# Norm crossings, TensorE fillers and first mixers of a two-block transformer kernel on one core: order of VectorE, ScalarE and GpSimd work

## The reference, cut to what matters

```
xn = rms_norm(x, attn_norm);  h = xn @ w_in          # split into latent, differential, grouped parts
latent (MLA): 6 heads;  differential: 4 heads x 2 maps, o = rms_norm((p0 - lam*p1) @ v);  grouped: 6 heads
x = x + concat(o_a, o_b, o_c) @ w_o
xn = rms_norm(x, ffn_norm);   x = x + (silu(xn@wg) * (xn@wu)) @ w_down        # 2816 wide
```

```
x = layer_norm(alpha*x + mixer(x));      # neighbourhood + sliding window attention, gated
x = layer_norm(alpha*x + f(x));          # f: dense 2816 in layer 0; 8 experts of 3584, top 2, in layer 1
```

## Time and profile before

| | |
|---|---|
| Time, median of 3 runs | 2284.98 us (2283.99 to 2286.79) |
| Profiled execution | 2285.07 us, span 2283.2 us |
| Mean granted TensorE clock | 0.987 |
| TensorE / VectorE / ScalarE / GpSimd busy | 97% / 75% / 65% / 10% |
| DMA | 569.32 MB, mean 249 GB/s |
| Stretches with a low granted clock (us) | 80-86, 128-136, 432-440, 484-488, 723-730, 907-911, 1098-1102, 1276-1290 |

### The profile page before, as it was taken

How to read it: one execution, slowest core, us unless ns; L and a number is a source line. 1 busy time by engine, 2 the same in 40 slices (tenths; PEclk the granted TensorE clock), 3 DMA queues, 4 the chain that set the end, 5 groups by cost and what they waited for, 6 DMA issues and landing times.

```text
span 2283.2 us, 30956 instructions
## 1 busy us (share of the span) xinstructions
PE 2211.2 (97%) x11540; PEld 1865.9 (82%) x11540; DVE 1708.3 (75%) x2448; ACT 1481.1 (65%) x2166; POOL 229.8 (10%) x140
## 2 busy tenths in 40 slices
PE   8889999899999999999999999999999999999997
PEld 7878888787887997888889788888888888888886
DVE  6866557866556547555646799999999999999998
ACT  6655446665444564444456588777787787888886
POOL 1430000330002241000251000000000000000000
PEclk9999999999999999999999899999999999999999
DMA  7426555425555544655544599999999999999996
GB/s 286 136 82 202 186 189 197 147 67 186 186 192 172 194 139 161 195 189 185 198 148 139 187 349 371 353 358 349 363 357 367 356 359 357 365 361 375 361 374 236
DMA packets 156844, 569.32 MB, mean 249 GB/s; under 512 B 18512, under 2 KB 18864, under 8 KB 156048
## 3 DMA queue, kind: packets, MB, share of 16 engines
q1 hardware_dynamic: 153600, 554.00, 68.5%
q0 software_dynamic: 3088, 13.27, 1.7%
HBM read 566.15 MB, written 1.05 MB: 248 GB/s over the span
## 4 chain that ended last, share of the span: by engine, by line
PE 74%; DVE 3%; ACT 1%; issue 1%; POOL 0%; DVEq 0%; ACTq 0%; POOLq 0%
PE bank L510 20%; PE bank L512 20%; PE bank L511 20%; PE bank L2220 3%; PE bank L2221 3%; PE bank L2222 3%; PE bank L1808 1%; PE bank L1065 1%; PE bank L2897 1%; PE bank L1080 1%; DVE X L2091 1%; PE bank L1007 1%; PE bank L2828 1%; DVE X L2050 0%; PE bank L2876 0%
## 5 line engine op out<-in xcount | busy, mean ns | idle before, releaser
L447 DVE TENSOR_TENSOR w_lo<-raw,w_hi 128x1024 fp32r<-128x1024 f32 x987 | 1190.2, 1224 | 278.1 <-ACT w_hi L441 246.2
L441 ACT CAST w_hi<-raw 128x1024 fp32r<-128x1024 f32 x1052 | 1098.8, 1051 | 314.1 <-PE bank L512 263.6
L510 PE MATMUL bank<-w_hi,x_hi 128*128 128x512 f32 (+2 forms) x2144 | 836.7, 390 | 16.1 <-DVE x_lo L2122 7.9
L512 PE MATMUL bank<-w_hi,x_lo 128*128 128x512 f32 (+2 forms) x2144 | 826.1, 385 | 0.0
L511 PE MATMUL bank<-w_lo,x_hi 128*128 128x512 f32 (+2 forms) x2144 | 824.9, 385 | 0.0
L510 PEld LDWEIGHTS bank<-w_hi,x_hi 128*128 128x128 f32 x2144 | 405.2, 189 | 95.9 <-POOL w_lo L447 8.8
L512 PEld LDWEIGHTS bank<-w_hi,x_lo 128*128 128x128 f32 x2144 | 405.4, 189 | 79.1
L511 PEld LDWEIGHTS bank<-w_lo,x_hi 128*128 128x128 f32 x2144 | 406.0, 189 | 73.2
L447 POOL TENSOR_TENSOR w_lo<-raw,w_hi 128x1024 fp32r<-128x1024 f32 x65 | 155.3, 2394 | 577.2 <-ACT w_hi L441 572.4
L512 PE MATMUL bank<-w_hi,qk_l 128*128 128x512 f32 (+1 forms) x496 | 191.9, 387 | 0.0
L510 PE MATMUL bank<-w_hi,qk_l 128*128 128x512 f32 x448 | 178.5, 398 | 0.5 <-DVE w_lo L447 0.5
(11 more groups left out here) (280 smaller groups left out, 2017.2 us busy)
## 6 DMA issues: line engine op xcount, KB each, us to landing
raw<-in_stream SPq DMA_DIRECT2D x1052, 512.0 KB, 5.7
tab<-in_lngb POOLq DMA_DIRECT2D x5, 1024.0 KB, 7.7
arena<-in_rpb POOLq DMA_DIRECT2D x16, 256.0 KB, 6.9
tab<-in_rowv POOLq DMA_DIRECT2D x2, 640.0 KB, 10.2
X<-in_x SPq DMA_DIRECT2D x1, 1024.0 KB, 5.0
out_y<-X SPq DMA_DIRECT2D x4, 256.0 KB, 2.6
tab<-in_ropec POOLq DMA_DIRECT2D x2, 448.0 KB, 5.4
tab<-in_ropes POOLq DMA_DIRECT2D x2, 448.0 KB, 7.8
```

Of the source, the lines that this page charges most:

```text
L441: nc.scalar.copy(w_hi[:, s % SPLIT, :], raw[:, slot, :]).then_inc(hi_done, 1)
L447: e.tensor_tensor(w_lo[:, s % SPLIT, :], raw[:, s % RAW, :], w_hi[:, s % SPLIT, :].bitcast(F32), ALU.subtract).then_inc(done, 1)
L510: pe.matmul(out, xh, wh, start=first, stop=False)
L512: return pe.matmul(out, xl, wh, start=False, stop=last)
```

## The change

- `pool_halves`: GpSimd has two halves (was three) at each entry of a second mixer and one (was three) at the dense network's; VectorE splits the others.
- `crossing`: GpSimd issues one split and then the pow of row block 1, ahead of the rest; VectorE's and ScalarE's splits are placed anew, and the middle normalising step of row block 1 stands between the two x_lo units of row block 0.
- `ln_add`: one tensor_scalar in place of two small instructions.
- `keep_busy`: TensorE matmuls of identity and X (f32, 256 columns) whose result nobody reads: five after the first transposes, five (three at the router) and one or three in each `crossing`, three and one around the router's choice, six on zeros at the very start.
- Start: ScalarE runs one Square on eight columns before the inputs are there.
- First mixers: in `fill`, GpSimd waits at steps 2, 4 and 6 for the scores of the map two further on, ahead of its split; `latent_heads(0)` after the last `diff_blocks`; ScalarE takes both column evacuations and the norm products.

```diff
-        own |= set(range(mixer2_at(l), mixer2_at(l) + 3))
-    own |= set(range(mixer2_at(0) + H_MIX2, mixer2_at(0) + H_MIX2 + 3))
+        own |= {mixer2_at(l), mixer2_at(l) + 1}
+    own.add(mixer2_at(0) + H_MIX2)
...
+            if first:
+                keep_busy(E, 5, 7)
...
+        def keep_busy(E, n, b):
+            if E.kind == "pe":
+                for _ in range(n):
+                    E.e.matmul(bank[b][:, 0:S], ident[:, :], X[:, 0, 0:S], start=True, stop=True)
...
                     e.wait_ge(acc_one, E.acc.at())
+                    e.wait_ge(acc_two, E.acc.at())
                     drain_dve(E)
...
-                if hx == 2:
-                    latent_heads(0)
...
             diff_blocks(2, 0)
+            latent_heads(0)
...
-                    if E.kind == "dve":
+                    if E.kind == "act":
                         need_rs(E, rows_made["norm", h0])
-                        e.tensor_tensor(x, x, scales(at, n, DV), ALU.mult).then_inc(qk_src, 1)
-                    E.qks.n += 1
+                        for tb in range(TB):
+                            for h in range(n):
+                                j = at + tb * n + h
+                                i = nc.scalar.mul(x[:, tb, h], x[:, tb, h], rs[:, j:j + 1])
+                        i.then_inc(dn_done, 1)
...
-                if E.kind in ("act", "dve"):
+                if E.kind == "act":
                     e.wait_ge(w_used, E.st.done(-1))
...
+                    for tb, taken in enumerate((acc_one, acc_two)):
+                        nc.scalar.mul(H[:, tb, c:c + n], bank[b + tb][:, 0:n], rsx[:, tb:tb + 1]).then_inc(taken, 1)
...
+                    if E.kind == "pool" and step in (2, 4, 6):
+
+                        e.wait_ge(s_full, E.map.at(step + 2) + 1)
...
-                E.link(e.tensor_tensor(negmu[:, tb:tb + 1], sx[:, 2 * tb:2 * tb + 1], sx[:, 2 * tb + 1:2 * tb + 2],
-                                       ALU.add))
-                e.tensor_scalar(negmu[:, tb:tb + 1], negmu[:, tb:tb + 1], -1.0 / D, None, ALU.mult).then_inc(
-                    mu_ready, 1)
+                e.tensor_scalar(negmu[:, tb:tb + 1], sx[:, 2 * tb:2 * tb + 1], sx[:, 2 * tb + 1:2 * tb + 2], -1.0 / D,
+                                ALU.add, ALU.mult).then_inc(mu_ready, 1)
...
+            entered = part is not None
             if E.kind == "pool":
 
                 e.wait_ge(tp_src, E.src.at(2))
-            if E.kind != "pe" and not later:
-                for _ in range(left - 1):
+                E.half_step()
+                ln_scale(E, 1)
+                for _ in range(left - 1 + entered):
                     E.half_step()
-                if E.kind == "pool":
-                    ln_scale(E, 1)
+            if E.kind == "act":
+                E.half_step()
                 E.half_step()
-            tb_blocks(E, 0, (0, 1))
+            if E.kind == "dve":
+                if entered:
+                    E.half_step()
+                tb_blocks(E, 0, (0, 1), units=(0,))
+                if entered and left == 3:
+                    E.half_step()
+                ln_mid(E, 1)
+                tb_blocks(E, 0, (0, 1), units=(1,))
+            else:
+                tb_blocks(E, 0, (0, 1))
...
             if E.kind == "pe" and routed:
                 logits(E, 0, base)
+                keep_busy(E, 3, 2)
+            else:
+                keep_busy(E, 5, 2)
             if E.kind == "pe" and part is not None:
                 halves(0, (0, 1))
+                keep_busy(E, *idle)
             if E.kind == "act":
                 ln_scale(E, 1)
-            ln_mid(E, 1)
+                for _ in range(left - 2 + entered):
+                    E.half_step()
             ln_last(E, 1)
-            if E.kind != "pe" and part is not None or later:
-                E.half_step()
+            if E.kind == "dve":
+                for _ in range(1 + entered):
+                    E.half_step()
             tb_blocks(E, 1, (6, 7))
...
                 logits(E, 1, E.tp.at(-2)).then_inc(lg_full, 1)
+                keep_busy(E, 3, 4)
...
+                keep_busy(E, 1, 4)
...
+                e.wait_ge(warm_set, 1)
+                nc.scalar.activation(arena[:, WARM:WARM + 8], arena[:, 0:8], ACT.Square)
...
+                e.memset(arena[:, 0:WARM], 0.0).then_inc(warm_set, 1)
...
+                e.wait_ge(warm_set, 1)
+                for _ in range(6):
+                    e.matmul(bank[7][:, 0:S], arena[:, 0:P], arena[:, P:P + S], start=True, stop=True)
```

More of the change, by code:

```diff
@@ L170 @@
 assert JUNK + TB * D <= B_SS
+WARM = P + S
 E_SIL = 0
@@ L405, in build @@
         hs_src, hs_done = sem("hs_src"), sem("hs_done")
+        dn_done = sem("dn_done")
+        warm_set = sem("warm_set")
         g_divided, gt_hi = sem("g_divided"), sem("gt_hi")
@@ L1572, in column_halves @@
                 E.acc.n += 1
-                if E.kind in ("act", "dve"):
+                if E.kind == "act":
                     e.wait_ge(w_used, E.st.done(-1))
-                if E.kind == "act":
-                    nc.scalar.mul(H[:, 0, c:c + n], bank[b][:, 0:n], rsx[:, 0:1]).then_inc(acc_one, 1)
-                if E.kind == "dve":
-                    e.tensor_scalar(H[:, 1, c:c + n], bank[b + 1][:, 0:n], rsx[:, 1:2], None, ALU.mult).then_inc(
-                        acc_two, 1)
+                    for tb, taken in enumerate((acc_one, acc_two)):
+                        nc.scalar.mul(H[:, tb, c:c + n], bank[b + tb][:, 0:n], rsx[:, tb:tb + 1]).then_inc(taken, 1)
             def out_half(n, done=0):
@@ L1631, in units @@
                     if E.kind == "pe":
-                        e.wait_ge(qk_src, made["diff01"])
+                        e.wait_ge(dn_done, 2 * l + 1)
                         e.wait_ge(acc_one, E.acc.at())
@@ L1643, in units @@
                     if E.kind == "pe":
-                        e.wait_ge(qk_src, made["diff23"])
+                        e.wait_ge(dn_done, 2 * l + 2)
                     out_unit(7, 5, 2, 2 * DH, scale=og_col[:, 0:1], lag=2)
@@ L1679, in fill @@
                     diff_norm(0, 2)
-                    made["diff01"] = E.qks.at()
                 if step == 10:
@@ L1692, in fill @@
                     diff_norm(DH // 2, 2)
-                    made["diff23"] = E.qks.at()
             def rows(at, n):
@@ L1750, in out_last @@
                 E.st.s += 2
-            tail = ffn(E, FF1 // FC, TB, scaled=True, enter=lambda part: rms_crossing(
+            tail = ffn(E, FF1 // FC, TB, scaled=True, enter=lambda part, idle=None: rms_crossing(
                 E, colg[:, l, CG_FFN:CG_FFN + KD], 2, out_last, part))
@@ L1963, in part @@
                     return i
-                enter(part)
+                enter(part, idle=(3, 4))
             else:
@@ L2129, in tb_blocks, with crossing @@
                 E.tp.n += 1
-        def crossing(E, alpha, tail, part, routed=False):
+        def crossing(E, alpha, tail, part, routed=False, idle=(1, 2)):
             e = E.e
@@ L2148, in crossing @@
                 ln_add(E, 1, alpha, bank[4:8])
-            later = E.kind == "dve" and part is None
+            entered = part is not None
             if E.kind == "pool":
                 e.wait_ge(tp_src, E.src.at(2))
-            if E.kind != "pe" and not later:
-                for _ in range(left - 1):
+                E.half_step()
+                ln_scale(E, 1)
+                for _ in range(left - 1 + entered):
                     E.half_step()
-                if E.kind == "pool":
-                    ln_scale(E, 1)
+            if E.kind == "act":
                 E.half_step()
-            tb_blocks(E, 0, (0, 1))
+                E.half_step()
[9 more added lines that the diff above has]
+                tb_blocks(E, 0, (0, 1))
             def halves(tb, hs):
@@ L2171, in crossing @@
                 logits(E, 0, base)
+                keep_busy(E, 3, 2)
+            else:
+                keep_busy(E, 5, 2)
             if E.kind == "pe" and part is not None:
                 halves(0, (0, 1))
+                keep_busy(E, *idle)
             if E.kind == "act":
                 ln_scale(E, 1)
-            ln_mid(E, 1)
+                for _ in range(left - 2 + entered):
+                    E.half_step()
             ln_last(E, 1)
-            if E.kind != "pe" and part is not None or later:
-                E.half_step()
+            if E.kind == "dve":
+                for _ in range(1 + entered):
+                    E.half_step()
             tb_blocks(E, 1, (6, 7))
-            if later:
+            if E.kind == "dve" and not entered:
                 E.half_step()
@@ L3027, in entering @@
             def entering(tail, alpha):
-                return lambda part, routed=False: crossing(E, alpha, tail, part, routed)
+                return lambda part, routed=False, idle=(1, 2): crossing(E, alpha, tail, part, routed, idle)
             for l in range(LAYERS):
```

## The result

The changed kernel takes 2274.11 us (median of 5 runs, 2269.88 to 2276.85), the kernel before 2285.75 beside it (2283.99 to 2286.79): a ratio of 0.9949, with a 95% interval of 0.9936 to 0.9963, or 11.6 us less. Forecast were 24.2 us less, 2260.8. The time lies in the range given (2251 to 2275), but less than half of the gain came. The profiled execution took 2274.11, span 2272.3, granted clock 0.992.

The account below looks back on a forecast made before the run. The prediction took TensorE, busy 2211.2 of 2283.2 us, as the bound, with its idle time and low clock to win. Terms 2.8 + 2.5 + 2.5 + 3.1 + 4.0 + 6.1 + 2.8 + 0.4 = 24.2 gave 2260.8 us, range 2251 to 2275.

Parts of the forecast that it names:

- Heads of the first mixers: First mixers: with the tables behind the differential units, L1291 and the first scores come 1.8 us earlier; -5.1 us together.
- only the first softmax step's distance counts: First mixers: moved tables stand before the first softmax step; second pair's softmax starts 2.0 us earlier in layer 0.
- further gain of 1.1 us in layer 1 from the low clock at 432 us: Layer 1's first mixer: low-clock stretch 432 to 440 lies behind the wait, so 3.1 us earlier against layer 0's 2.0.
- GpSimd's new waits: First mixers, steps 2, 4, 6: splits held for scores let VectorE go first; -1.4 us a layer, -2.8.
- the split falls on the next two-input instruction instead: First mixers: the low end for GpSimd's held-back splits, where they collide with a later VectorE instruction; gain 0.
- ScalarE's evacuations and products: First mixers: column evacuations and norm products moved from busier VectorE to ScalarE; -0.5 us a layer, ends +1.0 and -1.5.
- rival B: First mixers give nothing beyond the wait, as ScalarE is late for exponentials and copies; sum 15.3, 2270 us; chance 0.20.
- Crossings 1 to 3: Crossings into both second mixers (-2.5 us each) and into the dense network (-3.1): shorter chains, fillers holding the clock.
- Crossing 4: Crossing into the experts: mainly the clock held by fillers, speeding gather, transposes and router logits; -4.0 us.
- Rival C: Clock still falls in most crossings, so only shorter chains count; sum 12.8, 2272 us; chance 0.15.
- Start: Kernel start: early table load, fillers lifting the clock, faster transposes, earlier first weight matmul; -2.8 us, +1.3 to -3.5.

Follow-up runs that it names:

- e15: e8 with the first latent tables put back ahead of the differential units; 2268.88 us (0.9933).
- e8: e2 with eight TensorE fillers in each first mixer's attention, at steps 11 and 12; 2266.85 us (0.9918).
- e5: Changed kernel keeping only the tables' new place of its four first-mixer edits; 2271.22 us (0.9940).
- e1: Changed kernel with all four first-mixer edits undone; 2273.39 us (0.9946).
- e4: Changed kernel with only the first latent tables put back ahead of the differential units; 2277.15 us (0.9969).
- e16: e8 with GpSimd's splits at steps 2 and 4 held back until VectorE's products are done; 2261.01 us (0.9887).
- e12: e8 with ScalarE's new evacuations and products given back to VectorE; 2267.09 us (0.9918).
- e11: Changed kernel, GpSimd's waits kept, with eight fillers added in each first mixer's attention; 2266.27 us (0.9913).
- e7: Changed kernel without the fillers in the crossings and at the router, those of the start kept; 2275.54 us (0.9955).
- e6: Changed kernel without the start's edits (early fillers and ScalarE table load); 2277.30 us (0.9961).
- e13: e8 with GpSimd's split at step 2 alone held back until VectorE's products are done; 2265.97 us (0.9919).
- e2: Changed kernel without GpSimd's waits for the scores in the first mixers; 2269.59 us (0.9927).

## Why the prediction was wrong, point by point

**Heads of the first mixers, -5.1: the failed step.** The price of the wait itself was right (3.7 us in two layers). What failed is the sentence that of the rest only the first softmax step's distance counts. With the scores 1.8 us earlier, GpSimd's split of step 2, which had met L1411 before, meets the product behind it: L1426 takes 2.64 us for 0.56, the two products 3.99 for 2.90, and TensorE waited 4.8 us for the split output instead of 2.7. Worth of the move by the medians, and by the ratios to the kernel before: 2.0 and 3.4 us (e15 against e8), 2.2 and 1.4 (e5 against e1), 3.0 and 4.6 (e4 against the changed kernel), never the 5.1. My further gain of 1.1 us in layer 1 from the low clock at 432 us did not come either: that stretch went, and one of 3.4 us at 452 and 3.4 more at 483 came. In layer 0 the 3.4 us at 81 went, and 6.8 more came at 128.

**GpSimd's new waits, -2.8: the other failed step.** With them L1425 and L1433 gain what was forecast (2.34 to 1.35, 2.18 to 0.95; alone they take that, and not 1.2 both). But I had named "the split falls on the next two-input instruction instead" as the end worth 0. It happened at the first place in both layers and at the second in layer 0, and it is worth less than 0: 4.5 us lost without fillers, probably most of it by way of the clock, and with the fillers 0 by time and 2.2 by the two profiles. A wait for the scores is a wait for the wrong engine; waits for VectorE's products (e16) gave 5.8 us.

**ScalarE's evacuations and products, -1.0.** 0.2 with the clock held (e12), between -0.6 and +1.6 without. It was put beside work of VectorE that was not what TensorE waited for. ScalarE is late in one layer by 0.6 us at L1592 (in both in e11), which is rival B's sign, but not its mechanism: the exponentials are not late.

**Crossings 1 to 3, -8.1: right, 9.4.** The order came as described, and the mean and the pair at 0.21 and 1.41. The cause of the clock's part was wrong: I gave it to the fillers, and e7 keeps the clock and the gain without them. The shorter waits are the likely cause, which no run tests alone.

**Crossing 4, -4.0: too large.** In the changed kernel's profile it gains 2.2, in the others from 3.3 gained (e15) to 0.8 lost (e5), with the low clock from 3.4 to 13.7 us there. The fillers don't hold the clock here. The gather did come down, to 3.84 us from 6.26, when the clock was up:

```profile
1276.79 3.84 PE L2906 MATMUL bank<-arena,X 128*128 128x128 f32 x32 [0.49 <-DVE arena L2745]
```

Rival C describes this one crossing in part. Why the clock falls in some executions and not in others here stays open; no run tried more fillers at it.

**Start, -2.8: its chain came, its size is open.** The first weight matmul started at 11.36 instead of 12.90 and the transposes took 0.12 each, as forecast, and 3.4 us of low clock from 13 us on, which the list of stretches before leaves out, were gone. Of that 0.3 us are left at the seventeenth half in the changed kernel's profile, 0.3 to 1.7 in the others, and e6 says 3.2 by time. What I had not counted is that the weights' DMA can take the gain back, as it did at 25 us.

In the one pair of profiles the terms add up: 0.3 + 9.4 + 2.2 + 0.3 and 1.9 lost in the mixers are 10.3, and the spans differ by 10.9. Against the forecast of 24.2 the mixers are short by 10.8, the start by 2.5 and crossing 4 by 1.8, and crossings 1 to 3 gave 1.3 more. That 2274.11 lies inside the range is no merit of the mechanism: the high end came from rival C, the clock falling in the crossings, and in three of four it did not. Rival B had the right place (mixers that give nothing beyond the wait) but another cause.

## What to carry to other kernels

A wait that ends earlier moves everything behind it: before its gain is counted, go through the next few microseconds and see which VectorE product lands under which GpSimd split. To keep a split off a product, let GpSimd wait for that product and for the ones that follow it up to the next wait of TensorE, not for an event that happens near it. Put fillers only where the granted clock is low in the profile. Price an edit again with the clock held, and compare the mean clocks of the two kernels too, since here an edit that cost 4.5 us cost nothing measurable once the clock was held.

## What the runs showed of the hardware

- A VectorE product of two SBUF operands that starts under a GpSimd split ends 0.4 to 0.8 us behind it, so it does nearly all of its work once the split is over: 0.56 became 2.64 (the changed kernel), a pair of 0.61 became 2.77 (there too), 0.95 became 2.98 (e13). One that had begun before the split kept its 1.35, and the split took 3.06 (changed kernel) to 3.28 (e2) for 2.38. VectorE's passes from PSUM (L891) take 0.48 beside a split (e16, at 88.60) as without one.
- The Trainium skill (SBUF — State Buffer, "Who interferes with whom") says that a tensor_scalar can contend too. Here one on one column took 0.21 beside a split (L2067), another on 12 columns 1.11 in the changed kernel at 106 us and 1.83 at 462 us (L884, elsewhere 0.16): the traces bear it out for some of these instructions only, and no run here shows what tells them apart.
- Eight fillers (one 128x256 f32 matmul each, 2.32 us for five) in waits of 1 to 2 us kept the granted clock at 1.00 over 28 and 22 us in e11, in which it had been 0.76 and 0.84 in the changed kernel.
